# State-space scan of a hybrid encoder block: GpSimd's share moves to VectorE, in pairs of units, and TensorE adds two products

## The chip, the cores and the metric

The kernel runs on one core of one Trainium2 chip, in float32. The core has TensorE (PE in the rows: matmul, and PEld for its weight loads), VectorE (DVE), ScalarE (ACT), GpSimd (POOL) and SyncE (SP, which here only starts DMAs). The metric is device time in microseconds for one call, the median of three runs.

## The reference, cut to what matters

A block mixes 272 tokens (16 meta tokens and 256 real ones) by a state-space layer and by windowed attention side by side, merges both through sigmoid gates, and then runs a feed-forward part that gathers experts by index. The change lies in the state-space layer:

```python
def _s5_direction(u_g, a_re, a_im, bb_re, bb_im, c_re, c_im, reverse):
    bu_re = jnp.einsum('lgc,gpc->lgp', u_g, bb_re)
    bu_im = jnp.einsum('lgc,gpc->lgp', u_g, bb_im)
    ...
    _, _, h_re, h_im = lax.associative_scan(
        _complex_linear_combine, (ar, ai, bu_re, bu_im), reverse=reverse, axis=0)
    ...
    return jnp.einsum('lgp,gcp->lgc', h_re, cr) - jnp.einsum('lgp,gcp->lgc', h_im, ci)
```

There are 64 groups of 64 complex states and two directions, so 8192 complex recurrences h[t] = a h[t-1] + bu[t] of length 272. The result y, a gelu and a gated product follow.

## The kernel before, in words

All engines run one long program each, ordered by hand with semaphores. The work comes in this order: norm and transposes, the input projection, attention over 8 heads (to about 212 us), **the state-space stage** (212.6 to 676.2 us), then the gated products, the output projection and the experts (from about 900 us on).

The state-space stage treats 64 *units* of 128 states. Eight units (4 row strips of 32 channels, 2 directions) belong to one of CT = 8 tiles of 128 channels; `cc` is the tile modulo 2, and a loop body holds two tiles, 16 units (`RPL`). A complex recurrence is made real: the input is turned by the angle of a^t, scanned with the modulus |a| alone, and turned back. For unit t:

- `state_inputs` (TensorE, lines 1255 to 1257): six matmuls with 32 rows of contraction and 128 x 272 out, a high and a low part of weights and inputs for the real and the imaginary part, into one of two pairs of PSUM banks.
- `turns` and `cos_sin` (ScalarE, 515 and 523 to 526) with `angles` (VectorE, 862 and 866): the angle, rounded, its sine and cosine, into `trig`, four buffers.
- `input_products` (VectorE, 875 and 877): `pa` = bu x cos, `pb` = swapped bu x sin, 128 x 544 each, one operand from PSUM.
- `turn_inputs` (GpSimd, 373 and 374): `gin` = `pa` + `pb` and `pa` - `pb`, 272 each.
- `scans` (VectorE, 885): two scans of 272, `gin` into `gst`.
- `cos_products` (VectorE, 893): `oc` = cos x `gst`, 512; `turn_back` (GpSimd, 381): `os_` = sin x `gst`, 512.
- `real_parts` (VectorE, 901): `oc`[0] - `os_`[1], 256; the second half of `turn_back` (GpSimd, 385): `oc`[1] + `os_`[0], 256.
- `state_outputs` (TensorE, 1270): two float32 matmuls, 128 rows into 32 columns x 256, real and imaginary, recorded as two each.

`gst`, `oc` and `os_` lie in the tensor `hs2`, which the rows show as `hs`. Once per tile come `scalars` and `inputs_low` (VectorE, 846 to 854), `take_y` (VectorE, 908) and `out_matrices` (GpSimd, 358 to 367: four products and two differences of 256, which make `cp`, the output weights).

TensorE has other work in the stage too: `half_gate` (1212), eight float32 matmuls 128 x 128 x 256 per call (16 records), one call per unit. Each engine treats at step t the unit of its own lag: VectorE `angles` of t, products of t-1, scans and cosine products of t-2, real parts of t-3; TensorE the gate half of t-4, inputs of t, outputs of t-3. After the stage ScalarE's gelu (561) waits for the last `take_y`, and TensorE's next product (1109) for the gelu.

Of the kernel before, what the change touches and what calls it, by code (L numbers as in the profile page):

```python
# [59 lines left out]
def build(nc, W, keys, par, bw, cw, meta, x, gffn, gfin, u_tab, v_tab, out):  # L60
    top = ExitStack()
    with top:
# [77 lines left out]
        def in_hs2(at):  # L140
            return h2f[:, at * 4 * L:(at + 1) * 4 * L].rearrange("p (s r t) -> p s r t", s=2, r=2)
        gst, oc, os_ = in_hs2(0), in_hs2(1), in_hs2(2)
# [93 lines left out]
        s_vl = sem("s_vl")  # L236
        s_tb, s_abs, s_trg = sem("s_tb"), sem("s_abs"), sem("s_trg")
# [5 lines left out]
        s_re, s_im = sem("s_re"), sem("s_im")  # L243
# [26 lines left out]
        LAG = 4  # L270
        RPL = 2 * SPC
# [6 lines left out]
        def behind(b, t, k):  # L278

            return (b, t - k) if t >= k else (b - 1, t - k + RPL)  # L280

# [6 lines left out]
        def _(sp):  # L288
# [15 lines left out]
            with sp.Fori(0, CT // 2) as b:  # L304
                for cc in range(2):
                    sp.wait_ge(s_bu, SPC * (2 * b + cc) + 8)
# [23 lines left out]
        def _(pool):  # L330
            pool.sem_inc(s_cp, 4)
            pool.sem_inc(s_os, 4)
# [13 lines left out]

            def out_matrices(b, cc, part):

                ct = 2 * b + cc
                cre, cim = cwt[:, cc, :, 0, :], cwt[:, cc, :, 1, :]  # L350

                def co(k):
                    return scur[:, cc, k, :].rearrange("p (i o) -> p i o", o=1).broadcast_to([P, SPC, 32])
                if part == 0:
                    pool.wait_ge(s_scur, 2 * ct + 2)
                    pool.wait_ge(s_cw[cc], 16 * b + 16)
                    pool.wait_ge(s_cp, 2 * ct + 4)
                    pool.tensor_tensor(cs[:, 0], cre, co(2), ALU.mult).then_inc(s_cpl, 1)
                    pool.tensor_tensor(cs[:, 1], cim, co(3), ALU.mult).then_inc(s_cpl, 1)
                elif part == 1:  # L360
                    pool.tensor_tensor(cs[:, 2], cre, co(4), ALU.mult).then_inc(s_cpl, 1)
                    pool.tensor_tensor(cs[:, 3], cim, co(2), ALU.mult).then_inc(s_cpl, 1)
                else:
                    pool.wait_ge(s_cpl, 4 * ct + 4)
                    pool.wait_ge(s_y, SPC * ct + 8)
                    pool.tensor_tensor(cp[:, cc, 0], cs[:, 0], cs[:, 1], ALU.subtract).then_inc(s_cp, 1)
                    pool.tensor_tensor(cp[:, cc, 1], cs[:, 2], cs[:, 3], ALU.subtract).then_inc(s_cp, 1)

            def turn_inputs(b, t):
                s, n = t % 2, RPL * b + t  # L370
                pool.wait_ge(s_ab, 2 * n + 6)
                pool.wait_ge(s_gst, 2 * n + 2)
                pool.tensor_tensor(gin[:, s, 0], pa[:, s, 0], pb[:, s, 0], ALU.add).then_inc(s_gin, 1)  # L373
                pool.tensor_tensor(gin[:, s, 1], pa[:, s, 1], pb[:, s, 1], ALU.subtract).then_inc(s_gin, 1)

            def turn_back(b, t):

                s, n, kept = t % 2, RPL * b + t, slice(0, SEQ) if t % 2 else slice(META, L)
                pool.wait_ge(s_gst, 2 * n + 6)
                pool.wait_ge(s_re, n + 1)  # L380
                pool.tensor_tensor(os_[:, s, :, 0:SEQ], trig[:, t % 4, 1:2, kept].broadcast_to([P, 2, SEQ]),  # L381
                                   gst[:, s, :, kept], ALU.mult).then_inc(s_os, 1)
                pool.wait_ge(s_os, n + 5)
                pool.wait_ge(s_oc, n + 5)
                pool.tensor_tensor(oc[:, s, 1, 0:SEQ], oc[:, s, 1, 0:SEQ], os_[:, s, 0, 0:SEQ], ALU.add).then_inc(s_im, 1)

            def scan_body(b, first=False):
                for t in range(RPL):
                    if t >= 1 or not first:
                        turn_inputs(*behind(b, t, 1))  # L390
                    if t >= 2 or not first:
                        turn_back(*behind(b, t, 2))
                    if t % SPC < 3:
                        out_matrices(b, t // SPC, t % SPC)

            scan_body(0, first=True)
            with pool.Fori(1, BODIES) as b:
                scan_body(b)
            turn_inputs(*behind(BODIES, 0, 1))
            turn_back(*behind(BODIES, 0, 2))  # L400
            turn_back(*behind(BODIES, 1, 2))

# [26 lines left out]
        def _(act):  # L429
# [80 lines left out]
            def turns(b, t):  # L510
                n, cc = RPL * b + t, t // SPC
                if t % SPC == 0:
                    act.wait_ge(s_scur, 2 * (2 * b + cc) + 2)
                act.wait_ge(s_ang, n + 1)
                nc.scalar.activation(tb[:, t % 2, :], iota, ACT.Copy, scale=scur[:, cc, 0, t % SPC:t % SPC + 1]
                                     ).then_inc(s_tb, 1)
# [26 lines left out]
            def scan_body(b, first=False):  # L543
                for t in range(RPL):
# [3 lines left out]
                    if t % SPC == 0:  # L548
                        inputs_high(b, t // SPC)
# [952 lines left out]
```

## Time and profile before

| | |
|---|---|
| median of 3 runs | 2251.73 us (2250.52 to 2251.89) |
| span of the profiled execution | 2252.9 us |
| state-space stage in it | 212.6 to 676.2 us, 463.6 us |
| in the stage, VectorE busy | 442.2 us |
| in the stage, TensorE busy | 392.8 us |
| in the stage, GpSimd busy | 308.5 us |

In a row of the timeline the columns are: start in us, duration in us, engine, line, operation, out<-in, shape, count, and in brackets the engine's idle time just before and what ended it. A matmul shape 32*128 32x272 is 32 rows of contraction, 128 columns of weights and 272 columns that stream. PEclk is the granted TensorE clock as a share of 2.4 GHz: 1.00 is 2.4, 0.50 is 1.2.

### The profile page before, as it was taken

How to read it: one execution, taken by the hardware profiler on the slowest of the kernel's cores; microseconds unless marked ns; L12 is line 12 of the kernel's file. 1: busy time of each engine (PE TensorE's matmuls, PEld its weight loads, DVE VectorE, ACT ScalarE, POOL GpSimd, SP SyncE). 2: the span in 40 equal slices, each digit the busy share in tenths (PEclk: the TensorE clock that was granted, in tenths of full speed). 3: DMA queues.
4: the chain of work that ended last, by engine and by line, in shares of the span. 5: the costliest groups of instructions: out<-in, count | busy, mean ns of one | idle time of the engine just before them, and what ended most of it. 6: DMA issues, size and time to landing. Idle time of an engine off the chain costs nothing.

```text
span 2252.9 us, 22858 instructions
## 1 busy us (share of the span) xinstructions
PE 1870.8 (83%) x6912; PEld 1133.1 (50%) x6912; DVE 1500.0 (67%) x2341; ACT 414.4 (18%) x879; POOL 1018.6 (45%) x862
## 2 busy tenths in 40 slices
PE   6988788888899999997797798777777777777776
PEld 5977466566668988653353354232323232222222
DVE  5545999999994553656556566667666666666654
ACT  4332222222224343111011011000100000100001
POOL 2042666666661510344344345344444555555332
PEclk9998789998899999999999999999999999999999
DMA  4432122222224555899999999999999999999997
GB/s 163 169 106 100 38 80 85 76 79 82 84 93 150 183 183 199 344 421 421 417 417 417 400 398 406 422 421 422 414 421 421 419 421 422 422 422 422 421 422 301
DMA packets 92552, 659.13 MB, mean 293 GB/s; under 512 B 10288, under 2 KB 10288, under 8 KB 12976
## 3 DMA queue, kind: packets, MB, share of 16 engines
q0 software_dynamic: 73728, 536.90, 57.6%
q1 hardware_dynamic: 18752, 121.36, 14.8%
q8 instruction: 34, 0.56, 0.1%
q14 instruction: 38, 0.31, 0.0%
HBM read 656.13 MB, written 2.10 MB: 292 GB/s over the span
## 4 chain that ended last, share of the span: by engine, by line
PE 36%; DMA 29%; DVE 19%; issue 10%; POOL 3%; ACT 1%; DVEq 1%; POOLq 0%; ACTq 0%; SPq 0%
DMA uv<-u_tab,eid 29%; PE ps L1405 12%; DVE hs L885 4%; DVE hs L893 3%; PE ps L1212 3%; PE ps L1116 3%; PE ps L1118 3%; PE ps L1117 3%; PE ps L1355 2%; POOL uv L425 2%; DVE uv L1056 2%; DVE pb L877 1%; PE ps L1338 1%; PE ps L1339 1%; DVE pa L875 1%
## 5 line engine op out<-in xcount | busy, mean ns | idle before, releaser
L1405 PE MATMUL ps<-uv,dg 128*128 128x512 f32 x2048 | 958.7, 614 | 268.5 <-DVE dg L1062 261.1
L1056 DVE CUSTOM_DVE_ANT_0 uv<-uv,xn 128x2048 f32<-128x2048 f32 x256 | 586.9, 2293 | 381.0 <-DMA uv<-u_tab,eid 353.2
L1405 PEld LDWEIGHTS ps<-uv,dg 128*128 128x128 f32 x2048 | 379.7, 193 | 825.3 <-issue 465.4
L425 POOL DMA_INDIRECT uv<-v_tab,eid x256 | 268.4, 1048 | 611.0 <-PE ps L1405 351.5
L422 POOL DMA_INDIRECT uv<-u_tab,eid x256 | 340.1, 1328 | 201.6 <-issue 184.5
L653 ACT ACTIVATE ga<-av 128x1 f32<-128x1 f32 x256 | 51.9, 203 | 1186.5 <-DVE av L1056 1186.5
L1212 PE MATMUL ps<-hT,ring 128*128 128x256 f32 x1024 | 263.8, 415 | 0.0
L1212 PEld LDWEIGHTS ps<-hT,ring 128*128 128x128 f32 x1024 | 207.7, 208 | 55.9 <-issue 24.7
L705 DVE TENSOR_TENSOR low_ring<-ring,wh 128x2048 fp32r<-128x2048 f32 x43 | 107.2, 2497 | 76.6 <-ACT wh L444 76.5
L1062 DVE TENSOR_SCALAR dg<-prm,ga,gw 128x128 f32<-128x128 f32 x256 | 94.0, 367 | 66.3 <-ACT ga L653 32.6
L1270 PE MATMUL ps<-hs,cp 128*32 128x256 f32 x256 | 76.0, 425 | 66.7 <-DVE hs L901 66.6
L444 ACT ACTIVATE wh<-ring 128x2048 fp32r<-128x2048 f32 x52 | 99.6, 1914 | 146.2 <-PE ps L1118 107.5
L885 DVE TENSOR_TENSOR_SCAN hs<-scur,gin 128x272 f32<-128x272 f32 x128 | 118.8, 968 | 0.0
L893 DVE TENSOR_TENSOR hs<-trig,hs 128x512 f32<-128x512 f32 x64 | 111.4, 1741 | 0.0
L373 POOL TENSOR_TENSOR gin<-pa,pb 128x272 f32<-128x272 f32 x64 | 65.1, 1017 | 96.8 <-DVE pb L877 95.8
L1355 PE MATMUL ps<-h2T,ring 128*128 128x256 f32 x448 | 100.8, 379 | 0.0
L381 POOL TENSOR_TENSOR hs<-trig,hs 128x512 f32<-128x512 f32 x64 | 92.1, 1439 | 9.6 <-DVE hs L885 9.6
L1355 PEld LDWEIGHTS ps<-h2T,ring 128*128 128x128 f32 x448 | 85.0, 190 | 21.8 <-issue 11.5
L1116 PE MATMUL ps<-hH,wh 128*128 128x272 f32 (+1 forms) x288 | 87.3, 303 | 5.7 <-DVE low_ring L705 4.5
L344 POOL TENSOR_TENSOR low_ring<-ring,wh 128x2048 fp32r<-128x2048 f32 x8 | 36.6, 4574 | 109.2 <-ACT wh L444 109.2
L1117 PE MATMUL ps<-hL,wh 128*128 128x272 f32 (+1 forms) x288 | 84.4, 293 | 0.0
L1118 PE MATMUL ps<-hH,low_ring 128*128 128x272 f32 (+1 forms) x288 | 84.3, 293 | 0.0
(245 smaller groups left out, 2342.0 us busy)
## 6 DMA issues: line engine op xcount, KB each, us to landing
ring<-W SPq DMA_DIRECT2D x104, 1024.0 KB, 4.8
uv<-u_tab,eid POOLq DMA_INDIRECT x256
uv<-v_tab,eid POOLq DMA_INDIRECT x256
xn<-x SPq DMA_DIRECT2D x2, 1024.0 KB, 6.4
bwt<-bw SPq DMA_DIRECT2D x8, 256.0 KB, 4.8
cwt<-cw SPq DMA_DIRECT2D x8, 256.0 KB, 5.0
out<-xn SPq DMA_DIRECT2D x4, 512.0 KB, 5.2
keyt<-keys SPq DMA_DIRECT2D x1, 1024.0 KB, 7.5
```

Source lines behind the costliest of these rows:

```text
L422: pool.indirect_dma_start(uv[:, s, 0, :], None, u_tab, at).then_inc(s_u[s], 16)
L425: pool.indirect_dma_start(uv[:, s, 1, :], None, v_tab, at).then_inc(s_vv[s], 16)
L705: nc.vector.tensor_tensor(low_ring[:, n % RING, :], ring[:, n % RING, :], high_slot(n), ALU.subtract).then_inc(s_low, 1)
L885: nc.vector.tensor_tensor_scan(gst[:, s, k, :], r, gin[:, s, k, :], 0.0, ALU.mult, ALU.add).then_inc(s_gst, 1)
L893: nc.vector.tensor_tensor(oc[:, s, :, 0:SEQ], trig[:, t % 4, 0:1, kept].broadcast_to([P, 2, SEQ]), gst[:, s, :, kept], ALU.mult).then_inc( ...
L1056: nc.vector.tensor_tensor_reduce(uv[:, j % UV, 0, :], uv[:, j % UV, 0, :], xn[:, T, :], 1.0, 0.0, ALU.mult, ALU.add, av[:, hh, j:j + 1]).t ...
L1116: nc.tensor.matmul(dst, wh[:, block0 + k, :], xh(k), start=(k == 0), stop=False)
L1117: nc.tensor.matmul(dst, wh[:, block0 + k, :], xl(k), start=False, stop=False)
L1118: ins = nc.tensor.matmul(dst, wl[:, block0 + k, :], xh(k), start=False, stop=(k == last))
L1212: ins = nc.tensor.matmul(ps[:, q % 2, 0:SEQ], w[:, k, :], hTv[:, k, META:L], start=(k == 0), stop=(k == KT - 1))
L1355: ins = nc.tensor.matmul(ps[:, 4 + q % 2, 0:SEQ], w[:, k, :], h2T[:, k, :], start=(k == 0), stop=(k == KT - 1))
L1405: ins = nc.tensor.matmul(ps[:, 4 * T + n, :], dg[:, j % 2, :], uv[:, j % UV, 1, n * 512:(n + 1) * 512], start=False, stop=last and i == 2 ...
```

## The change

- VectorE takes a **pair** of units (strips 2jp and 2jp+1 of one direction, `place` and `units`) in each instruction: 32 pairs, 4 per tile (`PPC`), 8 per loop body (`PPL`).
- GpSimd has no work left in the loop. `turned_inputs`, both products of `turned_back` and `out_matrices` are VectorE's. The scans work in place in `pa`; `gin` and `gst` are gone.
- The sum `oc`[1] + `os_`[0] is no longer made. `state_outputs` runs three products for each unit (real part, cos x imaginary, sin x real) and lets PSUM sum them.
- Of the inputs there is one buffer of four PSUM banks for a pair, where there were two of two banks for a unit; `state_inputs` takes the two units of a pair in turn. TensorE runs a gate's two halves at both ends of a step, with inputs and outputs between them.
- `angles` rounds a product that ScalarE has made, instead of making it again; sine and cosine are 544 wide; `trig` has two buffers.

```diff
         def behind(b, t, k):
-            return (b, t - k) if t >= k else (b - 1, t - k + RPL)
+            return (b, t - k) if t >= k else (b - 1, t - k + PPL)
...
             def angles(b, t):
-                nc.vector.tensor_scalar(tb[:, 2, :], iota, scur[:, t // SPC, 0, t % SPC:t % SPC + 1], MAGIC,
-                                        ALU.mult, ALU.add).then_inc(s_vl, 1)
...
+                nc.vector.tensor_scalar(rnd[:, :, :], tb[:, s, :, :], MAGIC, None, ALU.add).then_inc(s_rnd, 1)
+                dve.wait_ge(s_rnd, n + 1)
+                nc.vector.scalar_tensor_tensor(ang[:, s, :, :], rnd[:, :, :], MAGIC, tb[:, s, :, :],
                                                ALU.subtract, ALU.subtract).then_inc(s_ang, 1)
             def input_products(b, t):
                 dve.wait_ge(s_trg, 2 * n + 2)
+                dve.wait_ge(s_bu, n + 1 + PPL)
+                dve.wait_ge(s_os, n + 2)
+                bu = ps[:, 2:6, 0:L].rearrange("p (u r) t -> p u r t", u=2)
...
+                nc.vector.tensor_tensor(pa[:, :, :, :], bu, turn(0), ALU.mult).then_inc(s_ab, 1)
+                nc.vector.tensor_tensor(pb[:, :, :, :], bu[:, :, ::-1, :], turn(1), ALU.mult).then_inc(s_ab, 1)
+            def turned_inputs(b, t):
+                dve.wait_ge(s_ab, 2 * n + 4)
+                nc.vector.tensor_tensor(pa[:, :, 0, :], pa[:, :, 0, :], pb[:, :, 0, :], ALU.add).then_inc(s_gin, 1)
+                nc.vector.tensor_tensor(pa[:, :, 1, :], pa[:, :, 1, :], pb[:, :, 1, :], ALU.subtract).then_inc(s_gin, 1)
             def scans(b, t):
+                for k in range(2):
+                    dve.wait_ge(s_gin, 2 * n + 1 + k)
+                    for u in range(2):
+                        nc.vector.tensor_tensor_scan(pa[:, u, k, :], r, pa[:, u, k, :], 0.0, ALU.mult, ALU.add
+                                                     ).then_inc(s_gst, 1)
+            def turned_back(b, t):
+                dve.wait_ge(s_gst, 4 * n + 4)
+                dve.wait_ge(s_y, n - 1 + PPL)
+                nc.vector.tensor_tensor(oc[:, s], turn(0), pa[:, :, :, kept], ALU.mult).then_inc(s_oc, 1)
+                nc.vector.tensor_tensor(os_[:, s], turn(1), pa[:, :, :, kept], ALU.mult).then_inc(s_os, 1)
...
             def state_inputs(b, t):
                 pe.wait_ge(s_ab, 2 * n + 2)
                 for r in range(2):
-                    nc.tensor.matmul(dst, high, uh, start=True, stop=False)
-                    nc.tensor.matmul(dst, high, ul, start=False, stop=False)
-                    ins = nc.tensor.matmul(dst, low, uh, start=False, stop=True)
+                    for part in range(3):
+                        for u in range(2):
+                            ins = nc.tensor.matmul(ps[:, 2 + 2 * u + r, 0:L], w, x, start=(part == 0), stop=(part == 2))
             def state_outputs(b, t):
-                pe.wait_ge(s_re, n + 3)
-                pe.wait_ge(s_im, n + 1)
+                pe.wait_ge(s_re, n + 1)
+                for k, got in enumerate((oc[:, s, :, 0, :], oc[:, s, :, 1, :], os_[:, s, :, 0, :])):
+                    for u in range(2):
+                        ins = nc.tensor.matmul(ps[32 * j:32 * j + 32, 6 + cc, 0:SEQ], cp[:, cc, min(k, 1), 2 * j + way, :], rhs,
+                                               start=(way == 0 and k == 0), stop=(way == 1 and k == 2))
             def scan_body(b, first=False):
+                for t in range(PPL):
+                    if gated_now:
+                        half_gate(*behind(b, t, LAG), 0)
+                    state_inputs(*behind(b, t, 1))
+                    state_outputs(*behind(b, t, 3))
+                    if gated_now:
+                        half_gate(*behind(b, t, LAG), 1)
```

The order on VectorE in a step is now: `scalars` (first pair of a tile), products of t-2, real parts of t-3, `turned_inputs` and scans of t-2, `take_y` (last pair), `angles` of t, `turned_back` of t-2, `inputs_low` (first pair), a third of `out_matrices` (first three pairs). Every engine has LAG = 2 pairs where it had 4 units.

VectorE's program, one unit of a loop body before (`hs` is `hs2`; SCALAR_TENSOR_TENSOR at L885 is the scan):

```order
L885 SCALAR_TENSOR_TENSOR hs<-scur,gin 128x272 x2
L901 TENSOR_TENSOR hs<-hs 128x256
L891 REGISTER_ALU
L893 TENSOR_TENSOR hs<-trig,hs 128x2x256
L861 REGISTER_ALU
L862 TENSOR_SCALAR tb<-prm,scur 128x272
L866 SCALAR_TENSOR_TENSOR ang<-tb 128x272
L871 ISA
L872 REGISTER_ALU
L875 TENSOR_TENSOR pa<-ps,trig 128x544
L877 TENSOR_TENSOR pb<-ps,trig 128x544
```

The same engine after the change, most of one pair's step, down to the angles (the scan is at L868):

```order
L852 TENSOR_TENSOR pa<-ps,trig 128x1088
L853 TENSOR_TENSOR pb<-ps,trig 128x1088
L885 REGISTER_ALU
L887 TENSOR_TENSOR hs<-hs 128x2x256
L857 REGISTER_ALU
L858 TENSOR_TENSOR pa<-pa,pb 128x2x272
L859 TENSOR_TENSOR pa<-pa,pb 128x2x272
L865 REGISTER_ALU
L868 SCALAR_TENSOR_TENSOR pa<-scur,pa 128x272 x4
L836 REGISTER_ALU
L838 TENSOR_SCALAR rnd<-tb 128x544
L840 SCALAR_TENSOR_TENSOR ang<-rnd,tb 128x544
```

The step goes on with the turning back and, in a tile's third pair, the last part of the output weights:

```order
L879 TENSOR_TENSOR hs<-trig,pa 128x1024
L880 TENSOR_TENSOR hs<-trig,pa 128x1024
L828 ISA
L830 TENSOR_TENSOR cp<-cs 128x256
L831 TENSOR_TENSOR cp<-cs 128x256
```

What stood on GpSimd (two sums, the sine product, the output weights) now stands on VectorE, at twice the width; GpSimd's own sum at line 385 has no counterpart.

TensorE's program, one unit before (L1255 to L1257 are the inputs, L1270 the outputs, L1212 half a gate):

```order
L1255 MATMUL ps<-uP,bwH 128x272
L1256 MATMUL ps<-uP,bwH 128x272
L1257 MATMUL ps<-uP,bwL 128x272
L1255 MATMUL ps<-uP,bwH 128x272
L1256 MATMUL ps<-uP,bwH 128x272
L1257 MATMUL ps<-uP,bwL 128x272
L1270 MATMUL ps<-hs,cp 32x256 x2
L1212 MATMUL ps<-hT,ring 128x256 x8
```

and one pair after:

```order
L1252 MATMUL ps<-uP,bwH 128x272 x4
L1252 MATMUL ps<-uP,bwL 128x272 x2
L1252 MATMUL ps<-uP,bwH 128x272 x4
L1252 MATMUL ps<-uP,bwL 128x272 x2
L1266 MATMUL ps<-hs,cp 32x256 x6
L1206 MATMUL ps<-hT,ring 128x256 x16
```

Two units had 12 input, 4 output and 16 gate matmuls; a pair has 12, 6 and 16, and the gate's second half now stands next to the following gate's first.

## Rows read from the trace of the kernel before

**Rows 1.** Busy time by stage: the whole state-space stage, all engines.

```profile
core 0: us, PE busy (x) PEld busy (x) DVE busy (x) ACT busy (x) POOL busy (x), PEclk, DMA share, GB/s
212.60:676.20 463.60, 392.76 (x1619) 282.69 (x1620) 442.18 (x553) 120.62 (x306) 308.45 (x304) 0.87 0.21 76
```

**Rows 2.** Timeline of one unit amid the stage, VectorE and GpSimd.

```profile
450.53 1.84 DVE L885 TENSOR_TENSOR_SCAN hs<-scur,gin 128x272 f32<-128x272 f32 x2
450.77 1.02 POOL L373 TENSOR_TENSOR gin<-pa,pb 128x272 f32<-128x272 f32 x1 [0.38 <-DVE pb L877]
...
452.89 1.45 POOL L381 TENSOR_TENSOR hs<-trig,hs 128x512 f32<-128x512 f32 x1
453.13 1.75 DVE L893 TENSOR_TENSOR hs<-trig,hs 128x512 f32<-128x512 f32 x1
...
457.25 1.84 DVE L885 TENSOR_TENSOR_SCAN hs<-scur,gin 128x272 f32<-128x272 f32 x2
```

**Rows 3.** Timeline of VectorE at the stage's start, while GpSimd mostly rests.

```profile
212.65 0.18 DVE L846 COPY scur<-scal 128x48 f32<-128x48 f32 x1
213.07 0.82 DVE L862 TENSOR_SCALAR tb<-prm,scur 128x272 f32<-128x272 f32 x1
...
214.57 0.43 DVE L853 TENSOR_TENSOR uP<-ucur,uP 128x272 fp32r<-128x272 f32 x1
214.93 0.68 DVE L854 TENSOR_TENSOR bwL<-bwt,bwH 128x512 fp32r<-128x512 f32 x1
215.53 0.35 DVE L862 TENSOR_SCALAR tb<-prm,scur 128x272 f32<-128x272 f32 x1
215.91 0.44 DVE L866 SCALAR_TENSOR_TENSOR ang<-tb 128x272 f32<-128x272 f32 x1
217.66 0.72 DVE L875 TENSOR_TENSOR pa<-ps,trig 128x544 f32<-128x544 f32 x1 [1.31 <-PE ps L1257]
218.30 0.71 DVE L877 TENSOR_TENSOR pb<-ps,trig 128x544 f32<-128x544 f32 x1
```

**Rows 4.** Durations by line (min/median/max in ns), and two rows of the timeline.

```profile
L885 DVE TENSOR_TENSOR_SCAN hs<-scur,gin x128: 692/1169/1275, 221.4 to 667.5; 128x272 f32<-128x272 f32 x128
L901 DVE TENSOR_TENSOR hs<-hs x64: 394/910/918, 230.0 to 670.7; 128x256 f32<-128x256 f32 x64
L705 DVE TENSOR_TENSOR low_ring<-ring,wh x43: 2280/2293/10672, 30.2 to 879.4; 128x2048 fp32r<-128x2048 f32 x43
10.40 1.29 DVE L783 TENSOR_SCALAR gates<-xn,st 128x2048 f32<-128x2048 f32 x1
463.95 0.71 DVE L885 TENSOR_TENSOR_SCAN hs<-scur,gin 128x272 f32<-128x272 f32 x1
```

**Rows 5.** Timeline of TensorE at full clock, one unit and the start of the next.

```profile
453.48 0.39 PE L1255 MATMUL ps<-uP,bwH 32*128 32x272 f32 x1
453.71 0.28 PE L1256 MATMUL ps<-uP,bwH 32*128 32x272 f32 x1
453.83 0.28 PE L1257 MATMUL ps<-uP,bwL 32*128 32x272 f32 x1
...
454.42 1.05 PE L1270 MATMUL ps<-hs,cp 128*32 128x256 f32 x4
455.40 3.72 PE L1212 MATMUL ps<-hT,ring 128*128 128x256 f32 x16
459.05 0.39 PE L1255 MATMUL ps<-uP,bwH 32*128 32x272 f32 x1
```

**Rows 6.** Timeline of TensorE behind a wait at the turn of a tile.

```profile
266.37 1.91 PE L1270 MATMUL ps<-hs,cp 128*32 128x256 f32 x4 [3.92 <-DVE hs L901]
268.21 0.59 PE L1255 MATMUL ps<-uP,bwH 32*128 32x272 f32 x1
...
269.87 6.47 PE L1212 MATMUL ps<-hT,ring 128*128 128x256 f32 x16
276.27 0.39 PE L1255 MATMUL ps<-uP,bwH 32*128 32x272 f32 x1
```

**Rows 7.** Waits in the stage: who waited for whom, us in total, times, longest.

```profile
PE ps L1270 <- DVE hs L901: 66.6, 36, 7.7
DVE pa L875 <- PE ps L1257: 9.1, 12, 1.3
```

**Rows 8.** Timeline of the stage's end.

```profile
675.67 0.48 DVE L908 SCALAR_TENSOR_TENSOR yT<-ucur,scur,ps 128x256 f32<-128x256 f32 x1 [4.55 <-PE ps L1270]
676.18 1.91 ACT L561 ACTIVATE yT<-yT 128x2048 f32<-128x2048 f32 x1 [4.35 <-DVE yT L908]
```

**Rows 9.** Timeline of ScalarE at the stage's start.

```profile
215.18 1.28 ACT L524 ACT_TABLE_LOAD   x1
216.47 0.43 ACT L524 ACTIVATE trig<-ang 128x272 f32<-128x272 f32 x1
216.81 0.51 ACT L526 ACTIVATE trig<-ang,halfpi 128x272 f32<-128x272 f32 x1
```

More of the change, by code:

```diff
@@ L278, in behind, with place, units @@
         def behind(b, t, k):
-            return (b, t - k) if t >= k else (b - 1, t - k + RPL)
+            return (b, t - k) if t >= k else (b - 1, t - k + PPL)
+        def place(t):
+            return t // PPC, t % 2, t % PPC // 2
+        def units(t):
+            cc, way, jp = place(t)
+            return slice(4 * jp + way, 4 * jp + way + 3, 2)
         def flat(ap):
@@ L345, in _ @@
                                        wh1[:, q % 2, :], ALU.subtract).then_inc(s_lowq, 1)
[L347 to L399, printed above, removed]
@@ L547, in scan_body @@
                         cos_sin(*behind(b, t, 1))
-                    if t % SPC == 0:
-                        inputs_high(b, t // SPC)
-                    if t % 2 and (t >= LAG + 2 or not first):
-                        gate(*behind(b, t, LAG + 2))
+                    if t % PPC == 0:
+                        inputs_high(b, t // PPC)
+                    if t >= LAG + 1 or not first:
+                        gate(*behind(b, t, LAG + 1))
             scan_body(0, first=True)
@@ L934, in _ @@
                 scan_body(b)
-            input_products(*behind(BODIES, 0, 1))
             for t in range(2):
-                scans(*behind(BODIES, t, 2))
-                real_parts(*behind(BODIES, t, 3))
-                cos_products(*behind(BODIES, t, 2))
+                pair(BODIES, t)
+                turned_back(*behind(BODIES, t, 2))
             real_parts(*behind(BODIES, 2, 3))
@@ L1272, in state_outputs @@
                 ins.then_inc(s_y, 1)
             def scan_body(b, first=False):
-                for t in range(RPL):
-                    if t >= LAG + 2 or not first:
-                        half_gate(*behind(b, t, LAG))
-                    if t % SPC:
-                        state_inputs(b, t)
+                for t in range(PPL):
+                    gated_now = t >= LAG + 1 or not first
+                    if gated_now:
+                        half_gate(*behind(b, t, LAG), 0)
+                    if t >= 1 or not first:
+                        state_inputs(*behind(b, t, 1))
```

237 lines of the change are left out of this document (125 added, 112 removed).

## The prediction

> **What bounds the kernel now.** I read the busy times by stage first: in the state-space stage (463.6 us) VectorE is busy for 442.2 us, TensorE for 392.8 and GpSimd for 308.5 [rows 1]. VectorE sets the pace: two scan groups stand 6.72 us apart, one unit [rows 2], and TensorE waits 66.6 us in all for VectorE's real parts, while VectorE waits only 9.1 us for TensorE's inputs [rows 7]. The stage ends when `take_y` lets the gelu start [rows 8]; everything behind hangs on that one point, so a microsecond taken from the stage is one off the whole.
>
> Then I ask why a unit costs VectorE 6.7 us. The reader should lay its rows beside GpSimd's. The cosine product starts at 453.13 and takes 1.75 us; GpSimd's sine product runs from 452.89 to 454.34, and VectorE's ends at 454.88, 0.54 us behind, which is the time of its 512 elements alone [rows 2]. The second scan of a group likewise takes 1.17 us where one alone takes 0.69 to 0.71 [rows 4], and the real part 0.91 for 0.39. So VectorE's instructions with two SBUF operands stand still while a GpSimd instruction runs, and its products with an operand in PSUM (0.71, always) do not [rows 3]. I take this as the trace's reading, not as proven.
>
> **VectorE's part, step by step.** Undisturbed two-operand instructions take 0.43 us for 272 elements, 0.68 for 512 and 2.28 for 2048 [rows 3, 4]: 1.042 ns per element and 0.147 us fixed. The next one starts 0.07 to 0.08 us before the end (217.66 to 218.30 for 0.72) [rows 3], or about 0.04 us after it where it waits for it (0.35 long, 0.38 later). A scalar instruction goes from 0.35 (272) to 1.29 (2048), so 0.49 for 544. Per pair, start to start:
>
> - two products of 1088, 1.28 us each: 2.42
> - real parts, 512: 0.60
> - `turned_inputs`, two of 544 (was GpSimd's): 1.28
> - four scans, 0.71 each: 2.52
> - angles, 0.49 + 0.04 and then 0.72 - 0.08: 1.17
> - `turned_back`, two of 1024, 1.21 each, the second waited for by the next pair's product: 1.14 + 1.25 = 2.39
>
> Sum **10.38 us** for a pair, against 13.4 for two units. Once per tile: scalars 0.42, `inputs_low` 0.36 + 0.60, `take_y` 0.40, and the moved `out_matrices`, six of 256 elements at 0.34 = 2.04; together 3.82, so 11.3 us per pair on the mean. None of the moved work is free: VectorE is full, and all of it counts. What pays is the contention that goes and half of the fixed costs.
>
> Three edits I cost at nothing. ScalarE has two angle products, three 544-wide functions (by 0.43 us for 272 and 1.91 for 2048, some 0.66 each) and a gate per pair, about 3.5 us in 11 [rows 8, 9]; sine and cosine stand one step earlier than their use. The weight DMAs keep their distance in pairs (2 where it was 4 units), and at 0.21 busy the DMA engines have room [rows 1]. The single input buffer makes a loop of product (2.4 us) and inputs (1.7 us), 4.1 us inside a step of 11, so 7 us of unevenness fit in before it binds.
>
> The pipeline's start: scalars at 212.65, two angles, `inputs_low`, two thirds of `out_matrices`, and ScalarE's table load of 1.28 us before the first sine [rows 9] let the first pair's product start at about 219.2. From there 32 x 10.38, less 2 x 1.17 (no angles in the last two steps), plus 8 x 3.82 less the 2.7 already done, make 357.7 us: 576.9. Then the last real parts, 0.6, TensorE's six output matmuls, 2.7, `take_y`, 0.5, and hand-overs, 0.2: **580.9** where it is 676.15 now (675.67 + 0.48).
>
> **TensorE's part.** At full clock a unit takes 0.94 us for inputs (0.125 per matmul, 0.19 to change over), 0.98 for outputs (four records at 0.213; at half the clock the four take 0.86 more [rows 5, 6]) and 3.65 for a gate half, 5.57 together [rows 5]. A pair has twice the gates, 7.3; twelve input matmuls, 0.94 + 6 x 0.125 = 1.69; twelve output records, 0.98 + 8 x 0.213 = 2.69; less 0.1 for two gate halves in a row: **11.6 us** if every matmul takes its turn. That is the price of the third product: 0.85 us per pair. It lies above VectorE's mean of 11.3. But the new code lets neighbours differ: input matmuls alternate between two strips of 32 rows and two banks, output matmuls between two strips of 32 columns. No row of the trace shows two such neighbours, so the step is bounded by 11.6 above (none overlap) and 7.2 + 0.94 + 0.98 + 2 x 0.213 = 9.5 below (two at a time). Between these ends VectorE, at 11.3, sets the pace for all but the top 0.3 us; I take VectorE as the pace.
>
> The Trainium skill has a rule here: "TensorE: Matmul & The Clock Gate", Part 3 (Packing small matmuls), says that matmuls in different 32-row or 32-column tiles run at the same time, with 3.07x measured for four row tiles and 2.38x for three column tiles. By that rule the step is near the lower end and the time is the forecast's; by the rows alone, each matmul in its turn, it would be the first rival's. No row so far bears it out.
>
> **The clock.** Behind a wait of 3.9 us TensorE runs at 1.2 GHz for a while: outputs 1.84 us instead of 0.98, inputs 1.66 instead of 0.94, the gate half 6.40 instead of 3.65 [rows 6]. Those turns of a tile are where VectorE waits 9.1 us in all [rows 7]. With VectorE as the pace TensorE still waits 1 to 3 us in a step, so I charge half of it, 5 us (0 to 9): 585.9, a gain of **90 us**.
>
> Against its own time: span 2252.9 - 90 = 2163; the median of the runs lies 1.2 below the profiled span, so 2251.7 - 90 = **2161 us**. With neither clock loss nor any other, 2157.
>
> **Rivals.**
>
> *TensorE becomes the bound.* No overlap: the first inputs that matter follow the second pair's products, about 232.7; from there TensorE's steps of 11.6 us run to the end. 29 steps reach 569.1, then outputs, gate halves, outputs, half and last outputs add 20.8, a slow-clock start 4 and `take_y` 0.5: 594.4, a gain of 82, **2170 us**. For it: the rows as they stand, 11.6 over 11.3. Against: the alternation, which no row prices. Even a tenth of overlap hands the pace back to VectorE.
>
> *VectorE's steps are longer than the sum.* In-place scans, four-dimensional operands and waits on ScalarE are in no row in this form; 0.5 us per pair would be 16 us: **2177 us**, up to 2190.
>
> *The excess is not GpSimd's* (the change does not do what it says). If the slow forms are slow by themselves, the two 1024-wide products cost 3.4 each (1.75 for 512), scans 0.9, angles and real parts double: 10.4 + 6.8 = 17.2 per pair, and the stage ends near 800: **2375 us**, slower. It decides from some 2.9 us more per pair than my sum. Against it: a 512-wide instruction with two SBUF operands takes 0.68 at the stage's start [rows 3], and the ends of both engines' rows line up.
>
> *TensorE stays at 1.2 GHz.* A step would then be 12.8 + 3.0 + 5.3 = 21.1 us; all steps so would end the stage near 885. The change turns slower once a step's mean passes 14.4 us, 3 cold steps in 10. Half of them: **2310 us**. Against: full-speed stretches return within one gate half of steady work [rows 6], and TensorE's waits get shorter, not longer.
>
> **How the numbers follow.** VectorE as the pace, 2161: 0.52. TensorE as the bound, 2170: 0.32. Longer VectorE steps, 2177 to 2190: 0.10. Excess not GpSimd's: 0.02. Cold TensorE: 0.03. Something that brings it within 0.2% of before (about what a measurement tells from no change): 0.01. The range: below, no clock loss (2157) and 0.2 us less per pair: 2150. Above, the TensorE bound with 12 us of slow clock more: 2182. Slower by over 0.2%: 0.05, faster: 0.94.
>
> **What the changed profile would show.** VectorE's 1024-wide products at 1.21 us and scans at 0.70, each the same from first to last; real parts 0.68. Pair to pair 10.4 us, 11 to 12.5 at a tile's turn. GpSimd empty from 212 us to the end of the stage. If VectorE is the pace: TensorE waits at its input matmuls for `pb`, and output records stand closer than 0.213 us. If TensorE is: VectorE waits at `pa` for the inputs, once per pair. The prediction is wrong if the two-operand instructions keep their length without GpSimd, or if TensorE's clock in the stage falls below 0.8.

## The result and the profile after

The changed kernel takes **2151.35 us** (median of 4 runs, 2149.81 to 2152.23) against 2251.81 for the kernel before beside it (4 runs, 2250.52 to 2252.78): a ratio of 0.9553 with a 95% interval of 0.954 to 0.9567. That is 100.5 us less. The forecast was 2161, in a range of 2150 to 2182: the time lies in the range, 1.35 us above its lower end.

The stage by itself, as in [rows 1]: the window from the first copy of the scalars to the end of the last `take_y`. Columns: window, its length, then busy time and instructions of each engine, TensorE's granted clock, DMA share, GB/s.

```profile
core 0: us, PE busy (x) PEld busy (x) DVE busy (x) ACT busy (x) POOL busy (x), PEclk, DMA share, GB/s
212.56:572.26 359.70, 314.61 (x1760) 239.61 (x1760) 353.34 (x505) 105.89 (x209) 0.00 (x0) 0.94 0.28 100
```

VectorE is busy for 353.34 of 359.70 us, GpSimd for none. The stage ends at 572.26 instead of 676.15, 103.9 us earlier. Behind it nothing moved: the profiled span of 2148.0 leaves 1575.7 us after that point, and before it was 2252.9 - 676.15 = 1576.8. The two profiled spans are 104.9 us apart and the medians 100.5, because the median lies 3.3 us above the profiled span here and lay 1.1 below it before.

One pair of VectorE and the start of the next, to be laid beside the unit of [rows 2] (timeline: start, length, engine, line, operation, tiles):

```profile
384.97 1.28 DVE L852 TENSOR_TENSOR pa<-ps,trig 128x1088 f32<-128x1088 f32 x1
386.17 1.28 DVE L853 TENSOR_TENSOR pb<-ps,trig 128x1088 f32<-128x1088 f32 x1
387.37 0.68 DVE L887 TENSOR_TENSOR hs<-hs 128x512 f32<-128x512 f32 x1
387.97 0.71 DVE L858 TENSOR_TENSOR pa<-pa,pb 128x544 f32<-128x544 f32 x1
...
389.24 2.56 DVE L868 TENSOR_TENSOR_SCAN pa<-scur,pa 128x272 f32<-128x272 f32 x4
391.72 0.41 DVE L838 TENSOR_SCALAR rnd<-tb 128x544 f32<-128x544 f32 x1
392.17 0.73 DVE L840 SCALAR_TENSOR_TENSOR ang<-rnd,tb 128x544 f32<-128x544 f32 x1
392.81 1.22 DVE L879 TENSOR_TENSOR hs<-trig,pa 128x1024 f32<-128x1024 f32 x1
393.95 1.22 DVE L880 TENSOR_TENSOR hs<-trig,pa 128x1024 f32<-128x1024 f32 x1
395.08 0.42 DVE L825 TENSOR_TENSOR cs<-cwt,scur 128x256 f32<-128x256 f32 x1
...
395.75 1.28 DVE L852 TENSOR_TENSOR pa<-ps,trig 128x1088 f32<-128x1088 f32 x1
```

From 384.97 to 395.08 a pair without extras takes 10.11 us; two of the moved `out_matrices` instructions add 0.67. No row in it has an idle time. TensorE a little later in the stage, beside [rows 5]:

```profile
409.07 0.52 PE L1252 MATMUL ps<-uP,bwH 32*128 32x272 f32 x4 [0.99 <-DVE pb L853]
...
410.01 1.49 PE L1266 MATMUL ps<-hs,cp 128*32 128x256 f32 x12
411.43 7.17 PE L1206 MATMUL ps<-hT,ring 128*128 128x256 f32 x32
```

Twelve input matmuls take 0.94 us (409.07 to 410.01), as long as six did in [rows 5], and twelve output records take 1.42 (0.118 each), where four took 0.98 in [rows 5] (0.245 each, the change-over of about 0.13 counted in on both sides). With the gates' 7.17 a step is 9.5 us; once per tile one runs partly at the lower clock and takes 11.0 to 11.2 (see the clock charge below). The waits in the stage, beside [rows 7], in us in total, times, longest:

```profile
PE ps L1252 <- DVE pb L853: 38.4, 27, 3.0
...
DVE pa L852 <- DVE ucur L802: 2.0, 6, 0.4
```

VectorE's products at L852 never wait for TensorE; only the last `take_y` does, and that is in the rows of the stage's end, beside [rows 8]:

```profile
569.50 0.69 DVE L887 TENSOR_TENSOR hs<-hs 128x512 f32<-128x512 f32 x1
...
570.24 1.49 PE L1266 MATMUL ps<-hs,cp 128*32 128x256 f32 x12 [1.80 <-DVE hs L887]
571.78 0.48 DVE L894 SCALAR_TENSOR_TENSOR yT<-ucur,scur,ps 128x256 f32<-128x256 f32 x1 [1.59 <-PE ps L1266]
572.29 1.91 ACT L514 ACTIVATE yT<-yT 128x2048 f32<-128x2048 f32 x1 [11.05 <-DVE yT L894]
```

So VectorE sets the pace, as it did before; what changed is how long its instructions take and how many there are.

### The profile page after: what moved, and what is told of

Same layout as the page of the kernel before. It is cut to its first block, busy times and chain, and to the rows that moved or that the text cites. A ratio compares the mean times of both kernels' runs of the same rounds, so it can differ in the third digit from the quotient of the medians.

```text
span 2148.0 us, 22000 instructions
## 1 busy us (share of the span) xinstructions
PE 1790.8 (83%) x7040; PEld 1086.8 (51%) x7040; DVE 1411.5 (66%) x2293; ACT 399.7 (19%) x783; POOL 726.3 (34%) x558
## 4 chain that ended last, share of the span: by engine, by line
PE 34%; DMA 30%; DVE 20%; issue 10%; POOL 3%; ACT 1%; DVEq 1%; POOLq 0%; SPq 0%; ACTq 0%
DMA uv<-u_tab,eid 30%; PE ps L1406 14%; DVE pa L868 3%; PE ps L1356 3%; PE ps L1111 3%; PE ps L1113 3%; PE ps L1112 3%; POOL uv L376 2%; DVE uv L1051 2%; DVE pb L853 2%; DVE hs L880 2%; DVE hs L879 2%; PE ps L1339 1%; PE ps L1340 1%; PE ps L1338 1%
## 5 line engine op out<-in xcount | busy, mean ns | idle before, releaser
L373 POOL DMA_INDIRECT uv<-u_tab,eid x256 | 356.5, 1393 | 202.2 <-issue 184.1
L1206 PE MATMUL ps<-hT,ring 128*128 128x256 f32 x1024 | 237.0, 390 | 0.0
L1206 PEld LDWEIGHTS ps<-hT,ring 128*128 128x128 f32 x1024 | 196.9, 195 | 42.5 <-issue 15.8
L357 POOL TENSOR_TENSOR fresh<-gated 128x256 f32<-128x256 f32 x16 | 11.8, 739 | 452.2 <-DVE gated L958 452.2
L868 DVE TENSOR_TENSOR_SCAN pa<-scur,pa 128x272 f32<-128x272 f32 x128 | 82.0, 701 | 0.0
L1252 PE MATMUL ps<-uP,bwH 32*128 32x272 f32 x256 | 30.6, 326 | 42.6 <-DVE pb L853 38.4
L1111 PEld LDWEIGHTS ps<-hH,wh 128*128 128x128 f32 x288 | 56.7, 197 | 8.0 <-DVE low_ring L658 5.0
L1112 PEld LDWEIGHTS ps<-hL,wh 128*128 128x128 f32 x288 | 56.8, 197 | 0.4
```

Source lines behind the costliest of these rows:

```text
L373: pool.indirect_dma_start(uv[:, s, 0, :], None, u_tab, at).then_inc(s_u[s], 16)
L868: nc.vector.tensor_tensor_scan(pa[:, u, k, :], r, pa[:, u, k, :], 0.0, ALU.mult, ALU.add).then_inc(s_gst, 1)
L1111: nc.tensor.matmul(dst, wh[:, block0 + k, :], xh(k), start=(k == 0), stop=False)
L1112: nc.tensor.matmul(dst, wh[:, block0 + k, :], xl(k), start=False, stop=False)
L1206: ins = nc.tensor.matmul(ps[:, t % 2, 0:SEQ], w[:, k, :], hTv[:, k, META:L], start=(k == 0), stop=(k == KT - 1))
```

## The experiments

Eleven kernels beside the changed one. "Stage end" is the start of the gelu (676.2 before, 572.3 in the changed kernel); "expert part" runs from the start of the first expert dot to that of the last (1309.9 before, 1311.2 changed); both are of the profiled execution. Ratios are against the kernel before, with their 95% interval. Each kernel was run four times, the last two of the table twice.

| kernel | us, median | ratio | stage end | expert part |
|---|---|---|---|---|
| changed | 2151.35 | 0.9553 (0.954 to 0.9567) | 572.3 | 1311.2 |
| pool_busy | 2290.73 | 1.0173 (1.0156 to 1.019) | 708.8 | 1310.0 |
| units_vector | 2214.15 | 0.983 (0.9814 to 0.9847) | 636.7 | 1309.1 |
| inputs_in_turn | 2147.52 | 0.954 (0.952 to 0.956) | 569.3 | 1312.1 |
| outputs_in_turn | 2150.7 | 0.955 (0.9534 to 0.9566) | 571.8 | 1310.7 |
| all_in_turn | 2150.23 | 0.9545 (0.9529 to 0.9561) | 572.7 | 1310.9 |
| strips_apart | 2179.38 | 0.9668 (0.9652 to 0.9684) | 598.9 | 1312.4 |
| vector_sum | 2180.92 | 0.9679 (0.9663 to 0.9695) | 591.7 | 1321.6 |
| all_products | 2141.11 | 0.9507 (0.949 to 0.9523) | 552.8 | 1320.7 |
| all_products_round | 2126.98 | 0.9439 (0.9421 to 0.9457) | 548.1 | 1310.7 |
| all_products_pad16 | 2130.36 | 0.9454 (0.9435 to 0.9473) | 552.5 | 1309.9 |
| all_products_pad48 | 2145.36 | 0.952 (0.9501 to 0.9539) | 557.3 | 1322.3 |

**Is the excess GpSimd's?** The theory says that VectorE's instructions with two SBUF operands are slow only while GpSimd runs; the rival, that the forms are slow by themselves. Give GpSimd scratch work and leave the rest.

```diff
+            with pool.Fori(0, BODIES) as b:
+                for t in range(PPL):
+                    pool.wait_ge(s_gin, 2 * (PPL * b + t) + 1)
+                    for k in range(8):
...
+                        pool.tensor_tensor(o, x, y, f).then_inc(s_scr, 1)
```

> The changed kernel, with eight GpSimd instructions per pair added (two of each: 272, 272, 512 and 256 elements, two SBUF operands) that write a spare strip which nobody reads; they add nothing to the result. Theory (a GpSimd instruction and a VectorE instruction with two SBUF operands exclude each other): VectorE's scans and 1024-wide products grow again, to over 1.1 and over 2 us for some of them, its PSUM products stay at 1.28, and a pair costs 3 to 6 us more, 2250 to 2340 us in all. Rival (the forms of before were slow by themselves): scans stay at 0.70 us, the time stays within 5 us of 2151.

Rows of one pair, VectorE and GpSimd:

```profile
400.96 1.28 DVE L864 TENSOR_TENSOR pa<-ps,trig 128x1088 f32<-128x1088 f32 x1
...
404.83 9.71 POOL L364 TENSOR_TENSOR ukT<-prm 128x272 f32<-128x272 f32 x8 [4.42 <-DVE pa L870]
405.23 4.82 DVE L880 TENSOR_TENSOR_SCAN pa<-scur,pa 128x272 f32<-128x272 f32 x4
...
412.02 2.06 DVE L891 TENSOR_TENSOR hs<-trig,pa 128x1024 f32<-128x1024 f32 x1
...
416.22 1.28 DVE L864 TENSOR_TENSOR pa<-ps,trig 128x1088 f32<-128x1088 f32 x1
```

The four scans that took 2.56 us take 4.82 behind the start of GpSimd's eight instructions, the 1024-wide product 2.06 instead of 1.22; L870 and L871, which start before GpSimd does, are unchanged. A pair takes 15.3 us, the stage 136 us more, and the kernel is 1.7% slower than the one before. The instructions' own form is innocent. The product with an operand in PSUM keeps its 1.28 too, but that tells nothing here, since GpSimd rests while it runs. The trace of the kernel before tells it, where such a product ran beside GpSimd:

```profile
455.72 0.93 POOL L366 TENSOR_TENSOR cp<-cs 128x256 f32<-128x256 f32 x1
...
455.98 0.71 DVE L875 TENSOR_TENSOR pa<-ps,trig 128x544 f32<-128x544 f32 x1
```

All 64 products of L875 there take 0.709 to 0.726 us, 18 of them with GpSimd at work for a third of their time or more.

The Trainium skill ("SBUF — State Buffer", Who interferes with whom) gives the same rule as an exclusive lock: a VectorE instruction with two SBUF inputs and a GpSimd instruction that reads SBUF wait for each other's whole length. The trace agrees: from the first scan to the end of the second 1024-wide product VectorE needs 10.3 us (405.23 to 415.55) where the changed kernel needs 5.8 (389.24 to 395.08), with GpSimd's 9.71 us lying over them. Single instructions fit too: L891 starts at 412.02, one of GpSimd's runs from 411.59 to 412.99, and L891 ends 1.1 us behind that, about its undisturbed 1.22.

**How much is the port, how much the pairing?** The kernel before, with GpSimd's `turn_inputs` and `turn_back` done by VectorE unit by unit; GpSimd keeps `out_matrices`.

```diff
-                    if t >= 1 or not first:
-                        turn_inputs(*behind(b, t, 1))
-                    if t >= 2 or not first:
-                        turn_back(*behind(b, t, 2))
...
+                        turn_inputs(*behind(b, t, 1))
...
+                        sin_products(*behind(b, t, 2))
```

> The kernel before, unit by unit, with GpSimd's two input sums, its sine product and its imaginary sum moved to VectorE and nothing else changed; the output weights stay on GpSimd. It separates the freed port from the doubled width. By durations of undisturbed rows a unit costs VectorE about 5.9 us instead of 6.7, so 64 units give some 50 us: 2195 to 2205 us. Rival (the gain is from fewer, wider instructions alone): moving work to the full engine makes the unit longer, 6.7 + 2.3 us, and the time rises to about 2390 us.

```profile
405.68 0.72 DVE L852 TENSOR_TENSOR pa<-ps,trig 128x544 f32<-128x544 f32 x1
...
413.88 0.72 DVE L852 TENSOR_TENSOR pa<-ps,trig 128x544 f32<-128x544 f32 x1 [0.55 <-ACT trig L501]
...
415.15 0.98 DVE L830 TENSOR_TENSOR uP<-ucur,uP 128x272 fp32r<-128x272 f32 x1
416.06 1.21 DVE L831 TENSOR_TENSOR bwL<-bwt,bwH 128x512 fp32r<-128x512 f32 x1
...
422.90 0.72 DVE L852 TENSOR_TENSOR pa<-ps,trig 128x544 f32<-128x544 f32 x1 [1.07 <-PE ps L1256]
```

The rival's 2390 is out: with more work on the full engine and no wider instruction the kernel got faster. A unit without extras takes 5.82 us (399.86 to 405.68), so 11.64 for two against 10.11 for a pair: fixed costs halved and the imaginary sum given to TensorE. More goes at a tile's turn. From 405.68 the second product to come starts at 422.90, 17.2 us for two units, 5.6 more than two plain ones: 0.80 us of idle time before the scalars for which the profile shows no cause, the scalars and `inputs_low`, GpSimd's `out_matrices` slowing L830 and L831 (0.98 and 1.21 where the changed kernel has 0.43 and 0.69), and waits on ScalarE and TensorE. The run missed the expected 2195 to 2205 by 9 us, and the turns account for it: 64 units at 5.82 instead of 6.72 us would save 57.6, the stage got 39.5 shorter (636.7 for 676.2), so the turns, with the stage's start and end, cost 18 us more than before. This much of GpSimd's work taken back brings 38 us of the gain, the rest of the change (pairs, the third product, `out_matrices` on VectorE) about 63. What each of these three is worth by itself was not run apart, but for the third product below.

**Is it the overlap on TensorE?** Three kernels put one unit's matmuls behind the other's.

```diff
-                for r in range(2):
-                    for part in range(3):
-                        for u in range(2):
+                for u in range(2):
+                    for r in range(2):
+                        for part in range(3):
```

> The changed kernel with only the twelve input matmuls of a pair unit after unit. If row strips overlap by themselves, this group grows from 0.94 to about 1.7 us and the outputs stay at 1.42; TensorE's step is then 10.3 us against VectorE's 10.8, so the time stays within 4 us of 2151. If the overlap of row strips were no cause, the group stays at 0.94.

```diff
-                for k, got in enumerate((oc[:, s, :, 0, :], oc[:, s, :, 1, :], os_[:, s, :, 0, :])):
-                    for u in range(2):
+                for u in range(2):
+                    for k, got in enumerate((oc[:, s, :, 0, :], oc[:, s, :, 1, :], os_[:, s, :, 0, :])):
```

> The changed kernel with only the six output matmuls of a pair unit after unit. If column strips overlap by themselves, this group grows from 1.42 to about 2.7 us and the inputs stay at 0.94; TensorE's step is 10.8 us, level with VectorE's: 2151 to 2160 us. If column strips do not matter, the group stays at 1.42.

Both edits in one kernel:

> The changed kernel with TensorE's twelve input and six output matmuls of a pair in another order: all of the first unit, then all of the second, so that neighbours lie in the same strip of 32 rows or columns. Theory (neighbours in different strips run two at a time, 0.94 and 1.42 us, and this slack keeps VectorE the pace): the groups take 1.7 and 2.7 us, TensorE's step 11.6 us, TensorE becomes the bound, 2165 to 2175 us, VectorE waits at pa once per pair. Rival (the order doesn't matter, the groups are short for another reason): 1.0 and 1.5 us as before, 2151 us.

TensorE in the kernel with both in turn:

```profile
408.99 0.52 PE L1252 MATMUL ps<-uP,bwH 32*128 32x272 f32 x2 [0.41 <-DVE pb L853]
409.35 0.28 PE L1252 MATMUL ps<-uP,bwL 32*128 32x272 f32 x1
409.36 0.53 PE L1252 MATMUL ps<-uP,bwH 32*128 32x272 f32 x4
...
410.30 1.94 PE L1266 MATMUL ps<-hs,cp 128*32 128x256 f32 x12
412.17 3.07 PE L1206 MATMUL ps<-hT,ring 128*128 128x256 f32 x13
```

These three told less than they were made for. The inputs take 1.31 us (408.99 to 410.30) and the outputs 1.87 (410.30 to 412.17), not 1.7 and 2.7: the second unit's first matmuls start before the first unit's last ones (a row of four begins 0.01 us behind a row of one). The step is 10.4 us, still under VectorE's 11.1, and the time stays. They confirm only that 0.8 us more on TensorE costs nothing; the 2165 to 2175 us expected of both in turn did not come. So the units were set truly apart:

```diff
                     for u in range(2):
+                        if gated_now and u == 0:
+                            half_gate(*behind(b, t, LAG), 0)
...
+                        state_inputs(*behind(b, t, 1), u)
+                        state_outputs(*behind(b, t, 3), u)
+                        if gated_now and u == 0:
+                            half_gate(*behind(b, t, LAG), 1)
```

> The changed kernel, but TensorE's step is first gate half, inputs of the first unit, outputs of the first unit, second gate half, inputs of the second unit, outputs of the second unit: no two neighbouring groups of the pair are of different units. The two kernels in turn had shown that groups written in turn still overlap in part (12 input matmuls 1.31 us, 12 output records 1.87 us). Theory that it is this overlap which leaves VectorE the pace: with it gone the step is 7.17 of gates + 2 x 0.94 of inputs + 2 x 1.45 of outputs (the kernel before took 0.98 for four records) = 11.95 us, more than VectorE's mean step of 11.2. TensorE then sets the end: 32 x 11.95 = 382 us for the stage in place of 359.7, stage end 595 to 605 and a time of 2173 to 2190 us, VectorE waits at its first product for the inputs in most pairs. Rival, that TensorE has room even so: 2150 us, and VectorE waits for nothing. Second rival, that the groups overlap across the gates too: a step of about 9.5 to 10.5 us and 2150.

TensorE; below it a first product of VectorE, and what the product's line waited for from 216 to 580 us (total, times, longest):

```profile
404.15 0.52 PE L1253 MATMUL ps<-uP,bwH 32*128 32x272 f32 x2
...
405.11 1.48 PE L1268 MATMUL ps<-hs,cp 128*32 128x256 f32 x6
406.52 3.72 PE L1206 MATMUL ps<-hT,ring 128*128 128x256 f32 x16
410.17 0.52 PE L1253 MATMUL ps<-uP,bwH 32*128 32x272 f32 x2
...
416.18 0.52 PE L1253 MATMUL ps<-uP,bwH 32*128 32x272 f32 x2
```

```profile
417.23 1.29 DVE L852 TENSOR_TENSOR pa<-ps,trig 128x1088 f32<-128x1088 f32 x1 [1.15 <-PE ps L1253]
```

```profile
DVE pa L852 <- PE ps L1253: 23.1, 25, 1.5
```

Each unit's six input matmuls take 0.96 us and its six output records 1.41. The step is 12.03 us (404.15 to 416.18, expected 11.95), TensorE has no idle time in it, VectorE waits in 25 of 31 pairs, and the time is 28 us longer. This order also hands a pair's inputs over in two halves, but the single buffer is not what binds: the second product of one pair (L853, 406.42 to 407.70) frees it, and TensorE comes to the next inputs only at 410.17. The overlap is what keeps the third product off the path.

**What is the imaginary sum on TensorE worth?** First back to VectorE, one 512-wide addition per pair and two products on TensorE; then the opposite, the real parts to TensorE too, as a fourth product with negated weights; then also the rounding, by ScalarE.

```diff
+                nc.vector.tensor_tensor(oc[:, s, :, 1, :], oc[:, s, :, 1, :], os_[:, s, :, 0, :], ALU.add
+                                        ).then_inc(s_re, 1)
...
-                for k, got in enumerate((oc[:, s, :, 0, :], oc[:, s, :, 1, :], os_[:, s, :, 0, :])):
+                for k, got in enumerate((oc[:, s, :, 0, :], oc[:, s, :, 1, :])):
```

> The changed kernel with the imaginary sum made on VectorE (one more instruction of 512 elements, 0.60 us per pair) and four output matmuls per pair in place of six. Theory (VectorE is the pace and TensorE has slack): 32 x 0.60 = 19 us more, 2170 us, and what TensorE saves, 0.45 us per pair, brings nothing. Rival (TensorE is near the bound as well): less than 12 us more.

```diff
-                for k, got in enumerate((oc[:, s, :, 0, :], oc[:, s, :, 1, :], os_[:, s, :, 0, :])):
+                for k, (got, wk) in enumerate(((oc[:, s, :, 0, :], 0), (os_[:, s, :, 1, :], 2),
+                                               (oc[:, s, :, 1, :], 1), (os_[:, s, :, 0, :], 1))):
```

> The changed kernel carried one step on: the real parts too are left to TensorE, eight output matmuls per pair with a third, negated set of output weights; VectorE's real_parts (0.60 us per pair) is gone, one 256-wide difference per tile is added (0.33 us), and the rounding instruction stands between the products and their sums. If VectorE is the pace: 32 x 0.60 less 8 x 0.33 is 16.5 us less, 2135 us; TensorE's step rises from 9.5 to 10.0 us. If TensorE were the pace it would get slower, 2155 to 2165 us.

```diff
-                nc.vector.tensor_scalar(rnd[:, :, :], tb[:, s, :, :], MAGIC, None, ALU.add).then_inc(s_rnd, 1)
+                nc.scalar.activation(rnd[:, :, :], tb[:, t % 2, :, :], ACT.Identity, bias=magic[:, :]).then_inc(s_rnd, 1)
```

> The kernel all_products with the rounding of the angle moved from VectorE (0.45 us per pair) to ScalarE, which is busy 0.3 of the stage. If VectorE is still the pace: 14 us less than all_products, about 2120 us. But VectorE's step, some 9.7 to 9.8 us, then lies under TensorE's 10.0, so the gain should be cut short: 2122 to 2130 us, with VectorE waiting at pa.

In the stage the addition costs 19.4 us, as expected (32 x 0.60 = 19.2). The real parts gone bring 19.5, three more than the 16.5 expected: the rounding now has other work between it and the angles that need it, and takes 0.35 us start to start where it took 0.45. The rounding gone brings 4.7 more, a third of its forecast of 14 and less than the instruction's time: the stage rows

```profile
212.56:552.77 340.21, 318.51 (x1888) 242.74 (x1888) 334.09 (x481) 106.02 (x210) 0.00 (x0) 0.97 0.29 104
```

```profile
212.56:548.10 335.54, 317.09 (x1888) 242.30 (x1888) 325.16 (x446) 126.31 (x241) 0.00 (x0) 0.97 0.30 105
```

(real parts moved, then rounding moved too) show 8.9 us less work on VectorE for 4.7 us of time. With the rounding gone nothing stands between the second product and `turned_inputs`, which then start 1.31 us behind it instead of 1.20, and the second pair's angles wait 2.9 us for ScalarE: 32 x (0.35 - 0.11) - 2.9 = 4.8. TensorE's sixteen output records take 1.84 to 1.85 us; its step is 10.0 to 10.1, close under VectorE's mean of 10.4 and, with the rounding gone, 10.2. VectorE's first product waits for TensorE in neither kernel, though that was expected of the second.

But the totals did not follow the stage. `vector_sum` and `all_products` lost 10 us later (2180.92 where 2170 was expected, 2141.11 where 2135 was). `all_products_round` did not, and its 2126.98 lies in the expected 2122 to 2130 by luck: of the 14 us against `all_products` the stage gave 4.7 and the expert part the rest.

**Where do the 10 us in the expert part come from?** In `all_products` VectorE stands still at two expert dots for over 10 us with nothing that the profile shows it waiting for:

```profile
1648.49 2.29 DVE L1047 CUSTOM_DVE_ANT_0 uv<-uv,xn 128x2048 f32<-128x2048 f32 x1 [10.23 <-issue]
...
1812.50 2.29 DVE L1047 CUSTOM_DVE_ANT_0 uv<-uv,xn 128x2048 f32<-128x2048 f32 x1 [10.29 <-issue]
```

Two kernels shift its instructions by repeating one memset at the program's start.

```diff
             step(nc.vector.memset(halfpi[:, :], HALF_PI))
+            for _ in range(16):
+                step(nc.vector.memset(halfpi[:, :], HALF_PI))
```

> The kernel all_products with the first memset of VectorE issued 16 times more at the start of the program, far ahead of the stage. Its expert part took 1320.7 us from the first dot to the last, 10 us more than the changed kernel's 1311.2, with VectorE idle 33.2 us at five dots where it waited for nothing that the profile shows. Theory that this comes with where the instructions of the loop lie in the program: shifted by 16 steps the idle stretches move or go, and the expert part takes another time, nearer 1310 (total about 2133 us, with the memsets' few us on top). Rival, that it comes with the time at which the stage ends or the expert loads start: the memsets shift everything by some 3 us and the expert part keeps its 1320 us (total 2143 to 2145).

> As the kernel with 16 memsets more, with 48: the theory of placement expects an expert part between 1309 and 1322 us that differs from that of the 16 or of none by several us in at least one of the two; the rival expects 1320 in all three.

The waits of this kind in the expert part, in the order `all_products`, sixteen memsets, forty-eight:

```profile
DVE uv L1047 <- issue: 33.2, 5, 10.3
```

```profile
DVE uv L1049 <- issue: 15.3, 4, 5.6
```

```profile
DVE uv L1049 <- issue: 22.0, 4, 5.5
```

Sixteen memsets made the kernel 10.8 us *faster*: the same stage end (552.5), the two stops of 10 us gone, an expert part of 1309.9 us. Forty-eight bring it back to 1322.3. So these 10 us come with where the instructions lie, not with the change, nor with the time at which the stage ends. Nor is it the chip: these eleven kernels were measured on three chips, and on each of them one with a long expert part and some with a short one.

The kept traces let one look closer. The ten kernels with a short expert part have two stops of over 5 us of this kind at expert dots, the three with a long one have four. In each of these 32 stops a packet of the DMA queue named `instruction` starts 3.3 to 4.0 us after the stop begins; the two of over 10 us have a second one, 8.3 us in, and VectorE goes on 1.9 to 2.2 us behind the last. Over the expert part this queue moves 34 packets in the three slow kernels and 22 to 24 in the others. So the stops go with this queue's packets. That VectorE stands waiting for its own instructions there is the plain reading, but no run tests it by itself, nor why one placement has two stops more than another.

With these 10 us aside, the fourth product is worth about 20 us, and the addition on VectorE costs about 20.

## Why the prediction was right

**The bound and its cause** held: VectorE before, VectorE after, and its two-operand instructions at their undisturbed length (scans 0.70, 1024-wide products 1.22, real parts 0.68) once GpSimd is silent. `pool_busy` shows the cause rather than arguing it.

```profile
L868 DVE TENSOR_TENSOR_SCAN pa<-scur,pa 128x272 f32<-128x272 f32 x128 | 82.0, 701 | 0.0
...
L838 DVE TENSOR_SCALAR rnd<-tb 128x544 f32<-128x544 f32 x32 | 13.4, 420 | 1.1 <-ACT tb L469 1.1
```

(Groups of VectorE in the stage: instructions, busy us, mean ns, idle before.)

**The pair's sum** was 0.2 us too high: with its extras it averages 11.12 us (the four of a tile, 373.23 to 417.72), forecast 11.33. A plain pair takes 10.11 for 10.38: the angles 1.09 for 1.17 (the rounding was taken at 0.49 and is 0.42), the scans 2.48 for 2.52, and the last term counted 0.11 us for the next pair's wait, which `out_matrices` or other extras cover where they stand there. A tile's extras take 4.05 for 3.82. Over 32 pairs the 0.2 is 6.8 us. The first product came at 218.76 (forecast 219.2), and the last twelve output records took 1.5 us where 2.7 was put. With the hand-overs that is the 8.6 us between 580.9, the sum without clock loss, and 572.3.

**The clock charge** of 5 us was the other term that was off. TensorE does wait up to 3 us a step, 38.4 in 27 times, as foretold, and its granted clock is low at first: 0.79 of full from 216 to 261 us, 0.97 behind that.

```profile
216.00:261.00 45.00, 38.34 (x198) 0.79 0.14 48
261.00:572.26 311.26, 276.26 (x1564) 0.97 0.30 108
```

(Window, length, TensorE busy, clock, DMA.) The slow clock behind waits came, and not only at the start: once per tile, behind a wait of 1.65 to 2.19 us, part of a step runs at the lower clock (0.84 to 0.85 granted over the step), and it takes 11.0 to 11.2 us instead of 9.5. Here the outputs take 2.71 us instead of 1.42:

```profile
387.50 0.52 PE L1252 MATMUL ps<-uP,bwH 32*128 32x272 f32 x4 [2.18 <-DVE pb L853]
...
388.72 2.78 PE L1266 MATMUL ps<-hs,cp 128*32 128x256 f32 x12
```

But VectorE's products never waited for it. The slow stretches sank into TensorE's own waits: with them a step takes TensorE some 9.9 us on the mean against VectorE's 11.1; and the step from 387.50, like the slowest one (12.4 us from 231.61), came after a wait and left none before the next. The prediction had itself found that 7 us of unevenness fit in before the input buffer binds, and charged the clock all the same. With the 8.6 that makes 13.6 us at the stage's end and, with the 1.1 us behind it, 14.9 by the profiled spans; by the medians it is 9.65.

**The range** held narrowly, and with some luck: one of the four executions, the profiled one, took 2149.81. The lower end had been put at no clock loss and 0.2 us less per pair, and both came true; the output matmuls, 1.2 us shorter than put, came on top. The errors that count lie on one side.

**TensorE's step** lay on the lower bound, 9.5, not near the 11.6 that a third of the chances was put on. "Two at a time" is what the rows show for inputs (12 in the time of 6) and for outputs (12 records in 1.42 us, the 0.98 + 2 x 0.213 = 1.41 of the lower bound). The rule of the Trainium skill cited there ("TensorE: Matmul & The Clock Gate", Part 3) is borne out here; its weight should have been greater. How large the rival was is now known too: without the overlap 2179.38, where 2170 was worked out. Its step was 0.4 us longer than the 11.6 put there, since groups set apart change over once more each: inputs 2 x 0.96 = 1.92 for 1.69, outputs 2 x 1.41 = 2.82 for 2.69, and the 0.1 for two gate halves in a row was lost.

**The rival of longer steps** fell: in-place scans and four-dimensional operands cost nothing extra (0.70 and 1.22). **The rival of slow forms** fell by the first row of the result and by `pool_busy`. **A cold TensorE** did not come: the stage's mean clock rose from 0.87 to 0.94. The other signs came as listed: a pair at a tile's turn takes 11.74 us (373.23 to 384.97), forecast 11 to 12.5.

## What to carry to other kernels

When two engines look busy side by side, lay the end of each slow row beside the other engine's rows: if the ends line up, the first engine also pays for work given to the second, and taking it back can be the gain. Price narrow matmuls strip by strip: neighbours in different strips share their time, so work moved from a full VectorE to TensorE can be free; `all_products_round` goes on that way, at 2126.98 us against 2151.35, and leaves TensorE's step 0.1 us under VectorE's. And when a total does not follow the stage that was changed, compare the parts that should be alike, and shift the code before believing a difference of half a per cent.

## What the runs showed of the hardware that was not expected

- Strips overlap even when one unit's matmuls are written behind the other's: 1.31 us for twelve inputs (0.94 alternating, 1.92 as two groups apart) and 1.87 for twelve output records (1.42 and 2.82).
- A TensorScalar instruction with one SBUF operand and a constant is held up by GpSimd as well: `rnd` takes 0.80 us on the mean in `pool_busy` and 0.42 without.
- The same stretch of 256 expert dots takes 1310 or 1321 us depending on some memsets added at the program's start, 0.8 ms ahead of it. With it go two or four stops of over 5 us, each with a packet of the instruction queue 3.3 to 4.0 us in.
